# Two-layer hybrid decoder in fp32 on one core: expert down products in column groups of 64 and 32, weights in whole row blocks, small products in halves

## The chip, the cores and the metric

The program runs on one core of a Trainium2 chip. The metric is device time in microseconds (us) of one execution, median of three runs. All arithmetic is fp32.

## The reference, cut to what matters

The input has 256 tokens of width 1024. Two layers each do a norm, one input projection, four kinds of token mixing (sliding-window attention, gated linear attention, stick-breaking attention, RWKV-7), an output projection and a second norm. Layer 0 then has a dense SwiGLU of width 2816, layer 1 a mixture of eight experts, of which each token uses two:

```python
def swiglu(h, w1, w3, w2):
    return (jax.nn.silu(h @ w1) * (h @ w3)) @ w2

def moe_swiglu(h, router, w1, w3, w2):
    ...
    for e in range(N_EXPERTS):            # 8 experts, w1 and w3 (1024, 1408), w2 (1408, 1024)
        out = out + combine[..., e:e + 1].astype(h.dtype) * swiglu(h, w1[e], w3[e], w2[e])
    return out
```

## The kernel before, in words

Each engine has its own hand-written program; semaphores tie them together. There are eight PSUM banks of 128 partitions by 512 floats. For a bank b the semaphore `full[b]` counts how often TensorE has filled it and `free[b]` how often it has been read out; `nth(i, b, k)` is the k-th such count in expert pass i, from the list `per` of uses per pass. `mm(out, lhsT, rhs)` (L518) is one product: the columns of lhsT (at most 128) are loaded as weights and the columns of rhs (at most 512) stream through. Nearly every matmul of the kernel has L518 as its line. In the trace a product is always two MATMUL records and two LDWEIGHTS records; I call each of these a record. In a row, "128*64 128x96" is a weight block of 128 rows by 64 columns and 96 streamed columns.

**Experts** (`experts(l)`, layer 1). A pass handles up to CAP = 96 token slots of one expert; with these inputs the loop runs eight times. The tokens of the expert are gathered with a one-hot matrix, `gather`: for each of eight feature blocks and two token tiles, two products of 64 weight columns with 96 streamed columns, into banks 6 and 7. They are scaled out into `slot_h` (ScalarE four blocks, VectorE four). Then come the stages of a pass, in TensorE's order:

1. *Up*: for each of 11 blocks j of 128 expert features, first the gate (w1), then the up side (w3): over eight blocks k of the model width, two products, one for weight columns 0 to 63 of the block and one for 64 to 127, with 96 streamed columns. Their outputs go to partitions 0 to 63 and 64 to 127 of bank j % 2. That is 11 x 2 x 8 x 2 = 352 products, 704 records. ScalarE takes the silu of each block and VectorE multiplies (`slot_act`), one block at a time beside TensorE.
2. *Transposes*: two, of the weights of the slots (`weigh`), into bank 2; ScalarE copies them to `weigh_t`.
3. *Gather* of the next expert: 32 products, 64 records.
4. *Down*: for each block k of 11, the 96 slots of `slot_act[:, k]` are the weight block (96 columns) and w2 streams in two halves of 512 columns, into banks 2 and 3: 22 products, 44 records.
5. *Scatter*: four products of 512 streamed columns that put the result back to tokens, after ScalarE and VectorE have copied banks 2 and 3 to `slot_y`; VectorE adds each to `x_sb`.

**Weights of the experts.** SyncE issues 18 pieces for each pass, into nine slots of 128 x 2176 floats (six of `ring`, three in `region_e`). A piece of w1 or w3 is 256 columns of all eight row blocks, so each of its packets is 1 KB; a piece of w2 is two whole row blocks, with packets of 4 KB. A slot is refilled when TensorE is through with it. The pieces of a pass are 17.3 MB.

**Mixers** (`layer_mixers(l)`, once for each layer). Several products there have 128 weight columns and only 64 streamed ones: CO 12 products, GO 8, AO 12, right-hand sides RH0 4 and RH1 8, solves U0 4 and U1 4, outputs Y0 8 and Y1 12, so 72 in a layer. BON (4 in a layer) streams 2 columns and the router RT (16, in layer 1 alone) streams 8. They stand between other work of 128 weight columns; only GO is followed by products of 64 weight columns (L745 ff.). In `layer_mixers` the product LW (weight rows 0 to 63, input `d_th` in `region_m`) stands as four records ahead of the four records of LA (rows 64 to 127, input in `region_e`).

Of the kernel before, what the change touches and what calls it, by code (L numbers as in the profile page):

```python
# [9 lines left out]
ALU = mybir.AluOpType  # L10
# [3 lines left out]
P = 128  # L14
HALF = 64
D = 1024
# [37 lines left out]
MAX_PASSES = -(-SEQ // CAP)  # L54

# [84 lines left out]
def psum_plan():  # L140
# [9 lines left out]
    for l in range(DEPTH):  # L150
# [19 lines left out]
        if l % 2 == 0:  # L170
            for j in range(D_FF // P):
                use(f"up{j}", l, j % 2)
            for i in range(4):
                use(f"dn{i}", l, 2 + i)
        else:
            for name, bank in (("RT", 6), ("POS", 7), ("G0", 6), ("G1", 7)):
                use(name, l, bank)
# [16 lines left out]
def build(nc, t_in, out):  # L194
    ctx = ExitStack()
    with ctx:
# [13 lines left out]
        ring = sb("ring", [P, SLOTS, SLOT])  # L210
        region_e = sb("region_e", [P, 8192])
        region_f = sb("region_f", [P, 4096])
        region_g = sb("region_g", [P, 3072])
        region_m = sb("region_m", [P, 5128])
        normed = sb("normed", [P, 2, 512])
        ar = sb("ar", [P, 2, 2, NT, 256])
        c_q = sb("c_q", [P, 2, 2, SEQ])
        b_q = sb("b_q", [P, 4, SEQ])
        b_att = sb("b_att", [P, NT, 4, P])
        a_k = sb("a_k", [P, 2, SEQ])  # L220
# [85 lines left out]
        final_row = region_f[:, 1024:2048]  # L306

        W = MAX_PASSES * N_EXPERTS + N_EXPERTS
        slot_act = region_e[:, 0:UPC * CAP].rearrange("p (c s) -> p c s", c=UPC)
        slot_silu = region_f[:, 0:2 * CAP].rearrange("p (b s) -> p b s", b=2)  # L310
        slot_h = region_m[:, 0:KC * CAP].rearrange("p (c s) -> p c s", c=KC)
        pick = region_m[:, 768:768 + NT * CAP].rearrange("p (t s) -> p t s", t=NT)
        weigh = region_m[:, 960:960 + NT * CAP].rearrange("p (t s) -> p t s", t=NT)
        weigh_t = region_m[0:CAP, 1152:1152 + SEQ].rearrange("p (t n) -> p t n", t=NT)
        slot_y = region_m[0:CAP, 1408:1408 + D]
        place = region_m[:, 2432:2432 + NT * W].rearrange("p (t i) -> p t i", t=NT)
        chosen = region_m[:, 2432 + NT * W:2432 + 2 * NT * W].rearrange("p (t i) -> p t i", t=NT)
        share = region_m[:, 2432 + 2 * NT * W:2432 + 3 * NT * W].rearrange("p (t i) -> p t i", t=NT)
        count = region_m[:, 3072:3072 + N_EXPERTS]
        most = region_m[:, 3080:3088]  # L320
# [58 lines left out]
        def slot(n):  # L379
            return n % SLOTS  # L380


        MORE = 3
        SLOTS_E = SLOTS + MORE
        more_slots = region_e[:, 8192 - MORE * SLOT:8192].rearrange("p (s n) -> p s n", s=MORE)
        more_landed = [ctx.enter_context(nc.semaphore(f"more_slot{i}_landed")) for i in range(MORE)]

        def expert_slot(k, n):

            r = k % SLOTS_E  # L390
            return ring[:, slot(FIRST_MOE + r), 0:n] if r < SLOTS else more_slots[:, r - SLOTS, 0:n]

        def expert_landed(i, k):

            r = k % SLOTS_E
            before = (FIRST_MOE + r) // SLOTS if r < SLOTS else 0
            s = landed[slot(FIRST_MOE + r)] if r < SLOTS else more_landed[r - SLOTS]
            return s, i * (16 * (E_PIECES // SLOTS_E)) + 16 * (before + k // SLOTS_E + 1)

# [4 lines left out]
        E_PIECES = 3 * UP2  # L404
        assert E_PIECES % SLOTS_E == 0


        per = [(UPC + 1) // 2, UPC // 2, 3, 2, 1, 1, 1, 1]
# [12 lines left out]
        def _(sp):  # L421
# [42 lines left out]
            def expert_piece(e, k):  # L464
                if k < 2 * UP2:
# [1473 lines left out]
```

## Time and profile before

| | |
|---|---|
| median of 3 runs | 1143.51 us (1140.59 to 1144.64) |
| the profiled execution, its own time | 1143.13 us |
| its span, first to last instruction | 1141.3 us |
| TensorE busy | 1102.5 us (97%) |
| VectorE, ScalarE, GpSimd busy | 285.3, 192.9, 61.4 us |
| chain that ended last | TensorE 95%, VectorE 3% |
| eight expert passes | 689.3 to 1131.6 us |
| HBM read | 211.67 MB |

Times in rows are microseconds from the start of the span. A TensorE group of the timeline runs from the start of its first record to the modelled end of its last, so the groups overlap a little; distances from start to start are what counts. The chain is followed back from the last instruction: each step goes to what released it.

### The profile page before, as it was taken

The page shows a single profiled execution, that of the slowest core. Times are in us where ns is not written, and L with a number is a line of the kernel's source. Part 1 is how long each engine was busy: PE and PEld are TensorE (multiplying, and loading weights), DVE is VectorE, ACT ScalarE, POOL GpSimd, SP SyncE. Part 2 cuts the span into 40 slices and gives each one's busy share as a digit, 9 for nine tenths or more (in the row PEclk, how much of TensorE's full clock was granted, in tenths as well). Part 3 has the DMA queues.
Part 4 walks back from the last instruction along what each step waited for, and adds up shares of the span by engine and source line. Part 5 has one row for each costly group of instructions (what it writes and reads, how often), then busy time and mean ns, then how long its engine had stood idle before and what let it go on. Part 6 is the DMA issues. An engine that isn't in the chain of part 4 may idle for free.

```text
span 1141.3 us, 22432 instructions
## 1 busy us (share of the span) xinstructions
PE 1102.5 (97%) x9790; PEld 837.2 (73%) x9790; DVE 285.3 (25%) x645; ACT 192.9 (17%) x444; POOL 61.4 (5%) x67
## 2 busy tenths in 40 slices
PE   8999999899999999999999969999999999999996
PEld 6887887488888543887789549595949494949592
DVE  4432473500000001233376341020111112021112
ACT  2244231100000001214323011011010111101011
POOL 2000411000000000000312100000000000000000
PEclk8999999999999999999999989999999999999998
DMA  9633101335554445343210256989898989899870
GB/s 325 196 122 105 43 1 38 111 117 160 160 159 167 156 148 155 119 135 109 74 38 1 74 185 203 343 279 351 287 344 289 343 293 323 305 301 332 279 272 37
DMA packets 168650, 213.34 MB, mean 187 GB/s; under 512 B 5120, under 2 KB 151200, under 8 KB 168480
## 3 DMA queue, kind: packets, MB, share of 16 engines
q1 hardware_dynamic: 166032, 210.29, 56.0%
q10 hardware_dynamic: 2576, 2.45, 0.7%
q8 instruction: 32, 0.52, 0.2%
q14 instruction: 10, 0.08, 0.0%
HBM read 211.67 MB, written 1.05 MB: 186 GB/s over the span
## 4 chain that ended last, share of the span: by engine, by line
PE 95%; DVE 3%; issue 1%; ACT 1%; POOL 0%; DMA 0%; DVEq 0%; POOLq 0%; ACTq 0%
PE bank L518 93%; PE bank L523 1%; DVE tok L1434 1%; POOL small L1343 0%; DMA x_sb<-in_x 0%; DVE b_att L1616 0%; DVE b_q L1413 0%; PE bank L1045 0%; DVE x_sb L1410 0%; PE bank L829 0%; ACT tok L1121 0%; DVE small L1425 0%; ACT hT L1133 0%; DVE hT L1410 0%; PE bank L797 0%
## 5 line engine op out<-in xcount | busy, mean ns | idle before, releaser
L518 PE MATMUL bank<-hT,ring 128*128 128x256 f32 (+1 forms) x1184 | 260.3, 382 | 0.0
L518 PEld LDWEIGHTS bank<-hT,ring 128*128 128x128 f32 (+1 forms) x1184 | 223.4, 189 | 36.1 <-issue 2.7
L518 PEld LDWEIGHTS bank<-region_m,ring 128*64 128x64 f32 x4096 | 170.3, 137 | 8.6 <-issue 8.6
L518 PE MATMUL bank<-region_m,ring 128*64 128x96 f32 x4096 | 173.7, 246 | 2.9 <-DVE region_m L1860 1.6
L518 PE MATMUL bank<-ring,region_e 128*96 128x512 f32 (+1 forms) x368 | 160.0, 594 | 0.0
L518 PEld LDWEIGHTS bank<-ring,region_e 128*96 128x96 f32 (+1 forms) x368 | 64.1, 176 | 89.5 <-issue 88.5
L518 PE MATMUL bank<-ring,hT 128*128 128x256 f32 (+1 forms) x448 | 127.8, 442 | 1.4 <-ACT hT L1138 1.4
L518 PE MATMUL bank<-region_e 128*128 128x128 f32 (+2 forms) x512 | 119.2, 384 | 0.0
L1410 DVE TENSOR_TENSOR region_e<-region_f,bank 128x96 f32<-128x96 f32 (+1 forms) x110 | 31.7, 288 | 341.7 <-ACT region_f L1318 198.9
L518 PEld LDWEIGHTS bank<-ring,hT 128*128 128x128 f32 x448 | 84.0, 190 | 35.7 <-issue 25.8
L518 PEld LDWEIGHTS bank<-region_e 128*128 128x128 f32 (+1 forms) x512 | 71.9, 191 | 46.9 <-issue 46.8
L518 PE MATMUL bank<-region_m,region_e 128*64 128x96 f32 x1536 | 66.1, 246 | 0.0
L518 PEld LDWEIGHTS bank<-region_m,region_e 128*64 128x64 f32 x1536 | 64.4, 137 | 0.0
L1318 ACT ACTIVATE region_f<-bank 128x96 f32<-128x96 f32 x88 | 22.1, 251 | 234.8 <-PE bank L518 234.8
L1343 POOL TENSOR_TENSOR small<-small 128x1 f32<-128x1 f32 (+1 forms) x18 | 18.6, 1034 | 800.5 <-DVE small L1425 738.8
L1410 DVE TENSOR_TENSOR x_sb<-x_sb,bank 128x512 f32<-128x512 f32 x44 | 30.3, 689 | 93.5 <-PE bank L518 93.5
L518 PE MATMUL bank<-region_f 128*128 128x128 f32 (+1 forms) x352 | 43.0, 275 | 0.0
L518 PEld LDWEIGHTS bank<-region_f 128*128 128x128 f32 x352 | 41.2, 192 | 1.6 <-issue 1.6
L1880 DVE COPY region_m<-bank 96x512 f32<-96x512 f32 x8 | 5.5, 686 | 144.4 <-PE bank L518 144.4
L1296 ACT ACTIVATE region_f<-bank 128x256 f32<-128x256 f32 x22 | 8.4, 384 | 138.6 <-PE bank L518 138.6
L518 PE MATMUL bank<-region_m 96*128 96x512 f32 x64 | 30.4, 617 | 0.0
L523 PE MATMUL bank<-consts,tok 128*128 128x128 f32 x96 | 17.0, 323 | 13.5 <-DVE tok L1434 13.5
(234 smaller groups left out, 715.0 us busy)
## 6 DMA issues: line engine op xcount, KB each, us to landing
ring<-in_moe_w SPq DMA_DIRECT2D x80, 1024.0 KB, 6.9
region_e<-in_moe_w SPq DMA_DIRECT2D x40, 1024.0 KB, 6.8
ring<-in_ffn_w SPq DMA_DIRECT2D x33, 1024.0 KB, 5.4
ring<-in_w_in SPq DMA_DIRECT2D x22, 1024.0 KB, 5.4
ring<-in_w_out SPq DMA_DIRECT2D x8, 1024.0 KB, 4.9
ring<-in_moe_w SPq DMA_DIRECT2D x16, 512.0 KB, 5.8
region_e<-in_moe_w SPq DMA_DIRECT2D x8, 512.0 KB, 4.0
ring<-in_w_in SPq DMA_DIRECT2D x2, 1088.0 KB, 5.5
```

The lines of the kernel that those rows point to most:

```text
L518: return nc.tensor.matmul(o, lhsT, rhs, start=start, stop=stop, skip_group_check=True)
L523: last = nc.tensor.transpose(bank(name, l)[:, cc * 256 + t * P:cc * 256 + t * P + P], tok[:, t, (2 * c2 + cc) * P:(2 * c2 + cc + 1) * P], ...
L1296: nc.scalar.activation(silu_tmp[:, j % 2, :], bank(f"up{j}", l)[:, 0:SEQ], ACT.Silu).then_inc(sem("silu"), 1)
L1318: nc.scalar.activation(slot_silu[:, b, :], banks[b][:, 0:CAP], ACT.Silu).then_inc(sem("moe_silu"), 1)
L1343: g.tensor_tensor(ap_out, ap_in, m_half[:, 0:n], ALU.pow).then_inc(sem("rstd_ready"), 1)
L1410: return v.tensor_tensor(o, a, b, op)
L1434: v.tensor_scalar(tok[:, t, s], x_sb[:, t, s], scale, None, ALU.mult).then_inc(sem("h_ready"), 1)
L1880: v.tensor_copy(slot_y[:, 512:1024], banks[3][0:CAP, :]).then_inc(free[3], 1)
```

## The change

1. *Down in column groups.* The 96 slots are split into 64 and 32. For the first 64 slots a product has 64 weight columns and 512 streamed ones (`down_wide`), one for each half of w2: the first goes to array columns 0 to 63 and partitions 0 to 63 of bank 5, the second to columns and partitions 64 to 127 of bank 6. For the last 32 slots a product has 32 weight columns and 256 streamed ones (`down_narrow`), four of them in four groups of 32 array columns. In blocks k = 0 to 7 both kinds follow each other; for k = 8, 9, 10 (TAIL) all narrow ones come first, then the wide ones.
2. *Order of a pass*: up, transposes, down, gather, scatter. The transposes use bank 5, which down uses too, so down now waits for ScalarE's copy `weigh_t`. The scatter uses banks 1 to 4.
3. *Up with k outermost.* All 22 blocks accumulate together in banks 0 to 4, so silu and multiplication come at the end of the stage, five blocks (480 columns) in one instruction.
4. *Weights.* Sixteen row blocks `rows_a` (w1 and w3, 128 rows x 1408 columns, packets of 5.6 KB) and `rows_b` (w2, six transfers with packets of 4 KB) hold a whole expert. They lie in one `arena` over all mixer buffers. A row block is refilled for the next expert when TensorE is through with it. For the first expert, rows 9 and up and all of w2 wait for `x_updated`, the others for ring slots.
5. *Small products in halves* (`mm_halves`): the mixer products named above and the router's are split into two of 64 weight columns. The number of products and records of up and gather stays the same.

```diff
+def mm_halves(o, lhsT, rhs, start=False, stop=False):
+    for q in range(0, P, HALF):
+        last = mm(o[q:q + HALF, :], lhsT[:, q:q + HALF], rhs, start=start, stop=stop)
+    return last
...
-                    mm(o[:, h * HD:(h + 1) * HD], a0[:, hh, 0:P], c_v[:, 0, v], start=(h == 0), stop=True)
+                    mm_halves(o[:, h * HD:(h + 1) * HD], a0[:, hh, 0:P], c_v[:, 0, v], start=(h == 0), stop=True)
...
-        per = [(UPC + 1) // 2, UPC // 2, 3, 2, 1, 1, 1, 1]
+        GATE = [(0, j * CAP) if j < 5 else (1, (j - 5) * CAP) if j < 10 else (4, 0) for j in range(UPC)]
+        UP = [(2, j * CAP) if j < 5 else (3, (j - 5) * CAP) if j < 10 else (4, CAP) for j in range(UPC)]
+        per = [2, 2, 2, 2, 2, 3, 2, 1]
...
             with sp.Fori(0, n * N_EXPERTS - 1) as i:
+                for k in range(ROWS_A):
+                    if k < ROWS_A - 2:
+                        sp.wait_ge(sem("moe_row_used"), i * (KC - 1) + k // 2 + 1)
+                    else:
+                        sp.wait_ge(full[3], nth(i, 3, 1))
+                    expert_row_a((i + 1) % N_EXPERTS, k)
+                for b in range(ROWS_B):
+                    if b < ROWS_B - TAIL:
+                        sp.wait_ge(sem("moe_w2_used"), i * (ROWS_B - TAIL) + b + 1)
+                    else:
+                        sp.wait_ge(full[6], nth(i, 6, 2))
+                    expert_rows_b((i + 1) % N_EXPERTS, b)
...
+                def down_wide(k, g):
+                    return mm(banks[5 + g][g * HALF:(g + 1) * HALF, :], slot_act[:, k, 0:HALF],
+                              rows_b[:, k, g * 512:(g + 1) * 512], start=(k == 0), stop=(k == UPC - 1))
+                def down_narrow(k):
+                    for c in range(4):
+                        last = mm(banks[6 - c // 2][c * QUARTER:(c + 1) * QUARTER, 0:GW], slot_act[:, k, HALF:CAP],
+                                  rows_b[:, k, c * GW:(c + 1) * GW], start=(k == 0), stop=(k == UPC - 1))
+                        if k == UPC - 1 and c % 2:
+                            last.then_inc(full[6 - c // 2], 1)
+                    return last
...
                 with pe.Fori(0, n_passes * N_EXPERTS) as i:
+                    pe.wait_ge(free[7], nth(i, 7, 0))
+                    pe.wait_ge(free[0], nth(i, 0, 0))
+                    for k in range(KC):
+                        pe.wait_ge(a_landed[2 * k], 16 * i + 16)
+                        for j in range(5):
+                            last = up_tile(GATE[j], k, 2 * k, j, k == 0 and j == 0)
...
+                    pe.wait_ge(sem("weighs"), i + 1)
+                    pe.wait_ge(free[5], nth(i, 5, 0))
+                    for t in range(NT):
+                        last = nc.tensor.transpose(banks[5][0:CAP, t * P:(t + 1) * P], weigh[:, t, :], ident)
+                    last.then_inc(full[5], 1)
+
+                    pe.wait_ge(free[5], nth(i, 5, 1))
                     pe.wait_ge(free[6], nth(i, 6, 0))
+                    for k2 in range(ROWS_B):
+                        pe.wait_ge(b_landed[k2], 16 * i + 16)
+                        if k2 == 0:
+                            pe.wait_ge(free[2], nth(i, 2, 1))
...
+                        if k2 < ROWS_B - TAIL:
+                            for k in (2 * k2, 2 * k2 + 1):
+                                for g in range(2):
+                                    down_wide(k, g)
+                                last = down_narrow(k)
+                            last.then_inc(sem("moe_w2_used"), 1)
+                    for k in range(2 * (ROWS_B - TAIL), UPC):
+                        down_narrow(k)
+                    for k in range(2 * (ROWS_B - TAIL), UPC):
+                        for g in range(2):
+                            last = down_wide(k, g)
...
                     pe.wait_ge(sem("picks"), i + 2)
+                    gather((nth(i, 7, 0), nth(i, 0, 1)))
+                    for b, t, half in SCATTER:
+                        if half == 0:
+                            pe.wait_ge(free[5], nth(i, 5, 3))
+                        else:
+                            pe.wait_ge(free[6], nth(i, 6, 2))
+                        pe.wait_ge(free[b], nth(i, b, 1))
...
+                        for b in (0, 1):
+                            act.wait_ge(full[b], nth(i, b, 1))
+                            nc.scalar.activation(slot_silu[:, 5 * b:5 * b + 5, :],
+                                                 banks[b][:, 0:5 * CAP].rearrange("p (c s) -> p c s", c=5),
+                                                 ACT.Silu).then_inc(free[b], 1)
...
+                        act.wait_ge(full[5], nth(i, 5, 1))
+                        nc.scalar.copy(weigh_t, banks[5][0:CAP, 0:SEQ].rearrange("p (t n) -> p t n", t=NT)).then_inc(
+                            free[5], 1)
...
-SCATTER = ((4, 0, 0), (5, 0, 1), (2, 1, 0), (3, 1, 1))
+SCATTER = ((1, 0, 0), (2, 1, 0), (3, 0, 1), (4, 1, 1))
```

## Rows read from the trace of the kernel before

**Rows 1.** The page: chain that ended last, shares of the span by engine.
```profile
PE 95%; DVE 3%; issue 1%; ACT 1%; POOL 0%; DMA 0%; DVEq 0%; POOLq 0%; ACTq 0%
```

**Rows 2.** The same chain in order of time: start, length, what.
```profile
689.28 25.54 PE bank L518 x613
714.82 1.37 issue
...
775.64 54.73 PE bank L518 x820
```

**Rows 3.** Timeline of TensorE in one expert pass: start, us, engine, group.
```profile
746.02 16.06 PE L518 MATMUL bank<-region_m,ring 128*64 128x96 f32 x384
...
771.15 4.13 PE L518 MATMUL bank<-region_m,ring 128*64 128x96 f32 x96
775.21 0.42 PE L1045 MATMUL bank<-consts,region_m 128*96 128x128 f32 x2
775.57 2.86 PE L518 MATMUL bank<-region_m,tok 128*64 128x96 f32 x64
778.36 10.54 PE L518 MATMUL bank<-ring,region_e 128*96 128x512 f32 x24
788.74 8.75 PE L518 MATMUL bank<-region_e 128*96 128x512 f32 x20
797.37 3.80 PE L518 MATMUL bank<-region_m 96*128 96x512 f32 x8
801.11 1.13 PE L518 MATMUL bank<-region_m,ring 128*64 128x96 f32 x22
```

**Rows 4.** Timeline of TensorE, LW (region_m) and LA (region_e), layer 1.
```profile
481.90 0.48 PE L518 MATMUL bank<-region_m,lora 64*128 64x256 f32 x1
481.91 0.48 PE L518 MATMUL bank<-region_e,lora 64*128 64x256 f32 x1
...
482.65 0.38 PE L518 MATMUL bank<-region_m,lora 64*128 64x256 f32 x1
482.66 0.38 PE L518 MATMUL bank<-region_e,lora 64*128 64x256 f32 x1
```

**Rows 5.** Timeline of TensorE around gated attention's scores, which alternate column halves.
```profile
576.48 0.44 PE L708 MATMUL bank<-consts,hT 128*128 128x128 f32 x2
576.85 1.08 PE L518 MATMUL bank<-b_q,hT 128*64 128x256 f32 x8
577.87 0.60 PE L518 MATMUL bank<-region_e 128*128 128x128 f32 x3
```

**Rows 6.** Timeline of all engines, end of up to start of down.
```profile
775.67 0.37 ACT L1321 COPY region_m<-bank 96x256 f32<-96x256 f32 x1
777.15 1.04 ACT L1303 ACTIVATE region_m<-bank,params 128x96 f32<-128x96 f32 x4 [1.11 <-PE bank L518]
```

**Rows 7.** Timeline of all engines, end of down and the scatter.
```profile
796.66 0.58 ACT L1328 COPY region_m<-bank 96x512 f32<-96x512 f32 x1 [18.47 <-PE bank L518]
797.36 0.30 PEld L518 LDWEIGHTS bank<-region_m 96*128 96x128 f32 x2 [0.74 <-issue]
797.52 0.69 DVE L1880 COPY region_m<-bank 96x512 f32<-96x512 f32 x1 [18.05 <-PE bank L518]
798.53 0.69 DVE L1410 TENSOR_TENSOR x_sb<-x_sb,bank 128x512 f32<-128x512 f32 x1 [0.32 <-PE bank L518]
```

**Rows 8.** Busy time by stretch, one expert pass: engines, clock, DMA share, GB/s.
```profile
746.00:801.10 55.10, 55.10 (x823) 40.36 (x822) 8.29 (x24) 6.03 (x18) 0.00 (x0) 1.00 0.94 316
```

**Rows 9.** DMA in 780 to 790 us (w1, w3 pieces) and 765 to 775 (w2).
```profile
DMA packets 3448, 3.48 MB, mean 348 GB/s; under 512 B 48, under 2 KB 3448, under 8 KB 3448
...
DMA packets 1030, 3.96 MB, mean 396 GB/s; under 512 B 63, under 2 KB 63, under 8 KB 1030
```

**Rows 10.** Timeline of TensorE: AO of layer 1 and what follows.
```profile
618.93 2.79 PE L518 MATMUL bank<-region_m,hT 128*128 128x64 f32 x24
621.56 0.66 PE L518 MATMUL bank<-region_e 128*128 128x128 f32 x4
```

**Rows 11.** Timeline: the router's products.
```profile
671.22 4.85 PE L518 MATMUL bank<-router_sb,hT 128*128 128x8 f32 x32 [1.05 <-ACT hT L1133]
```

More of the change, by code:

```diff
@@ L15 @@
 HALF = 64
+QUARTER = 32
+TAIL = 2
 D = 1024
@@ L1042, in experts @@
-                    pe.wait_ge(sem("weighs"), i + 1)
-                    pe.wait_ge(free[2], nth(i, 2, 0))
-                    for t in range(NT):
-                        last = nc.tensor.transpose(banks[2][0:CAP, t * P:(t + 1) * P], weigh[:, t, :], ident)
-                    last.then_inc(full[2], 1)
-                    pe.wait_ge(sem("picks"), i + 2)
-                    gather(i, (nth(i, 6, 0), nth(i, 7, 0)))
-                    pe.wait_ge(free[2], nth(i, 2, 1))
-                    pe.wait_ge(free[3], nth(i, 3, 0))
@@ L1314, in _ @@
                     with act.Fori(0, n_passes * N_EXPERTS) as i:
-                        for j in range(UPC):
-                            b = j % 2
-                            act.wait_ge(full[b], nth(i, b, j // 2 + 1))
-                            nc.scalar.activation(slot_silu[:, b, :], banks[b][:, 0:CAP],
-                                                 ACT.Silu).then_inc(sem("moe_silu"), 1)
-                        act.wait_ge(full[2], nth(i, 2, 1))
-                        nc.scalar.copy(weigh_t, banks[2][0:CAP, 0:SEQ].rearrange("p (t n) -> p t n", t=NT)).then_inc(
-                            free[2], 1)
@@ new lines, in _ @@
+                        nc.scalar.activation(slot_silu[:, 10, :], banks[4][:, 0:CAP],
+                                             ACT.Silu).then_inc(sem("moe_silu"), 1)
+                        act.wait_ge(full[5], nth(i, 5, 1))
+                        nc.scalar.copy(weigh_t, banks[5][0:CAP, 0:SEQ].rearrange("p (t n) -> p t n", t=NT)).then_inc(
+                            free[5], 1)
+                        act.wait_ge(full[6], nth(i, 6, 1))
+                        for c in range(2):
+                            last = nc.scalar.copy(slot_y[HALF:CAP, c * GW:(c + 1) * GW],
+                                                  banks[6][c * QUARTER:(c + 1) * QUARTER, 0:GW])
@@ L1324, in _ @@
+                        last.then_inc(free[6], 1)
+                        act.wait_ge(full[5], nth(i, 5, 3))
+                        nc.scalar.copy(slot_y[0:HALF, 0:512], banks[5][0:HALF, :]).then_inc(free[5], 1)
+                        act.wait_ge(full[7], nth(i, 7, 1))
                         for c in range(4):
-                            last = slots_in(c, 6)
-                        last.then_inc(free[6], 1)
-                        act.wait_ge(full[2], nth(i, 2, 2))
-                        nc.scalar.copy(slot_y[:, 0:512], banks[2][0:CAP, :]).then_inc(free[2], 1)
+                            last = slots_in(c, 7)
@@ L1329, in _ @@
+                        last.then_inc(free[7], 1)
             square_sums(2 * DEPTH)
```

304 lines of the change are left out of this document (149 added, 155 removed).

## Prediction, made before the changed kernel was run

> **What bounds the kernel now.** I read the page's chain first: TensorE holds 95% of it [rows 1]. The chain in order of time then says where its work is back to back. From 720.55 to 1131.71 us there are only TensorE records, 54.73 us to an expert pass; the one wait is 1.37 us in the first pass [rows 2]. The timeline splits a pass [rows 3]. It lasts 801.11 - 746.02 = 55.09 us: up 29.19 (to 775.21), transposes 0.36, gather 2.79, down 19.01, scatter 3.74. So a microsecond that TensorE loses or gains in a pass counts eight times. DMA is busy for 0.94 of a pass [rows 8], but nobody waits for it after the first one.
>
> **How a product is paid.** In down a record streams 512 columns in 19.01 / 44 = 0.43 us, that is 0.84 ns a column. In up 608 records lie between 746.02 and 771.15 [rows 3], 41 ns each, where 96 columns alone would take 80 ns: two products in different array columns run at the same time. The scores of gated attention show it for 256 columns: 8 records in about 0.86 us, 0.108 each, where 0.215 would be due alone [rows 5]. And the order is loose. LA's four records stand behind LW's four in the program, yet its first starts 0.01 us after LW's first and its last 0.01 after LW's last [rows 4]. So records queued for another part of the array pass those that wait for their own.
>
> A change of the column width costs extra. Gather has 64 records x 0.041 = 2.64 us of work and takes 2.79; the transposes have 2 x 0.1075 of 0.36 [rows 3]; around the scores it is 0.37 - 0.215 and 1.02 - 0.86 [rows 5]. That is 0.14 to 0.16 us for each change, the unhidden first weight load included.
>
> **Part 1, down.** Before: 19.01 us, with 96 of the 128 array columns in use. After, for each k: wide, two products of two records of 0.43, the two products abreast, 0.86 us; narrow, four products of two records of 0.215, four abreast, 0.43 us. Eleven k make 11 x 1.29 = 14.19 us. The unknown is the change between column widths of 64 and 32. Blocks 0 to 7 change 8 times to narrow and 7 times back, and the tail changes once: 16. The trace has no such change. The nearest rows are the changes between 64 and 96 or 128 columns, 0.14 to 0.16 with a first load of 64 to 128 columns in them [rows 3, 5]; loads of 32 and 64 columns are shorter, so I take 0.14, and as ends 0 (no drain between these two) and 0.18. So 16 x 0.14 = 2.24, down 16.43 us, **2.58 less in a pass**.
>
> This is where a rule speaks against the change. Column width 64 and 128 cost 0.15 us at each border here [rows 3]. The Trainium skill, page "TensorEngine Tiling (Array Packing)", section "Key Properties", says that changing the tiling mode, not just the tile, drains TensorE. By that rule all 16 changes are paid (down 16.4); without it none (14.2). The trace agrees for the widths that it has.
>
> **Part 2, the order of a pass.** Up to transposes, transposes to down, gather to scatter, scatter to up: four changes of width as before, down to gather has none, as gather to down had one. Down now waits for the copy of `weigh_t`. ScalarE began it 0.46 us after the transposes began and took 0.37 [rows 6]; with 0.1 for the semaphore TensorE goes on 0.93 us after 775.21 instead of 0.36: **+0.57**. Queued behind that wait are down and everything else of TensorE. ScalarE must be free for it: its last silus cover 96 and 480 columns; a 512-column copy takes 0.58 [rows 7], and the last bank of the gate side is full 1.65 us (40 records x 0.041) before up ends. That holds. VectorE multiplies 480 columns in about 0.69 [rows 7]; bank 2 is full 0.83 before up ends, so it is done before the copy; bank 3 is first needed four k later. Up to +0.4 if the silus come late. After down, gather's 2.64 us cover the copies to `slot_y` (0.58 and 0.69 [rows 7]); the 0.1 us which the scatter now loses at such a wait goes, and so does a first load, **-0.14**. The scatter's 3.6 us cover the scaling of the next slots (1.04 [rows 6]). VectorE's additions (0.69 each [rows 7]) free banks 1 to 4 in the order in which up asks for them; the fourth ends about 1 us into up, which asks for bank 4 only after 40 records (1.65 us). Nothing.
>
> **Part 3, up with k outermost.** The same 704 records; 29.19 us stays. Nothing (bounds: 0 to 0.3 for a few waits).
>
> **Part 4, weights.** With packets of 1 KB the DMA moved 348 GB/s at full share, with 4 KB 396 [rows 9]. A pass of 52.9 us needs 17.3 MB / 52.9 = 327 GB/s, below both; a row block is refilled nearly a whole pass ahead of its use. The first pass took 746.02 - 689.28 = 56.74 us, 1.65 more than the others [rows 2, 3]; that wait for weights goes, because SyncE queues everything by 666 us and 17.3 MB at 396 GB/s arrive long before their turn: **-1.7**. If not, 0.
>
> **Sum for the experts.** A pass: -2.58 + 0.57 - 0.14 = -2.15; eight: -17.2; with the first pass -18.9 us.
>
> **Part 5, halves.** AO's 24 records take 621.56 - 618.93 = 2.63 us, 0.11 each, though 64 columns stream in 0.054 [rows 10]: the load of 128 weight columns sets the pace. As halves each load is half as long, and up shows that the loads of the two halves run side by side (two serial ones of 0.055 would not fit a pair's 0.082 [rows 3]). So four records in 0.112 us instead of two in 0.223, -0.111 a product; the upper end of the pace is up's own, 0.041 a record, -0.058 a product. An excursion from width 128 to 64 and back costs 0.33 us: two drains of 0.09 and the first loads of 0.05 and 0.10. GO needs none, since 64-column products follow it. In a layer: CO, AO, Y1 (12 each) -1.0; GO -0.9; Y0, RH1 (8 each) -0.56; RH0, U0, U1 (4 each) -0.1; BON 0. That is -5.3, or -1.4 at the upper pace; two layers -10.6 or -2.8. The router's 16 products (4.85 us, partly at a lower clock [rows 11]) bring -1.4 or -0.6. Small waits take some of it, since other engines' chains then end last; I take **-10**, ends -12 and -3. The nearest row to small moving widths is up, whose pairs show parallel loads, so I stay near the lower end.
>
> **Total.** Against the profiled execution's own 1143.13 us (its span is 1141.3): -18.9 - 10 = 1114.2. That execution lies 0.4 us below the median, so 1114.6.
>
> **Rivals.** (a) *No drain between 64 and 32.* All 16 changes are free; another 8 x 2.24 = 18 us go: 1097 us. For it: both are column groups that keep all rows. Against it: every change of width in the trace is paid [rows 3, 5].
>
> (b) *Slower: the four narrow products do not run four abreast but two.* Then narrow costs 0.86 a k, down is 11 x 1.72 + 2.24 = 21.2 us, a pass grows by 2.15 + 0.57 - 0.14 = 2.6, eight by 21, and with -1.7 - 10 the sum is 1152.5. The side changes where the narrow k costs 0.43 + 28.9 / 88 = 0.76, some 2.3 abreast. For it: nothing in the trace runs more than two abreast, and were a record to start only after the one ahead of it, two records of one product would block the next group. Against it: rows 4, where records four places behind start with the first. The Trainium skill, page "TensorE: Matmul & The Clock Gate", section "The mechanism", says that matmuls keep strict program order; rows 4 disagree. By that rule the wide products still pair up, the narrow ones too, and this rival's time comes out.
>
> (c) *The gains are there but small*: changes at 0.18 us (16 x 8 x 0.04 = 5.1), late silus (8 x 0.4 = 3.2), the mixers at -3 (7): 1114.6 + 15.3 = 1130. This is the upper edge of the forecast.
>
> **Chances.** Forecast with its bounds (1105 to 1130) 0.68; (a), 1093 to 1103, 0.14; (b) 0.11; within 0.3% for other reasons 0.04; between 1130 and 1140 0.03. Range: 1097 to 1130. About 0.3% is what a measurement of this kernel tells from no change. Faster 0.85, same 0.04, slower 0.11.
>
> **What would show it.** In the timeline of a pass: up 29.2; 0.9 from transposes to down; down 16.4 (14.2 for (a), 21.2 for (b)), with 1.57 us from one k's first wide record to the next's; gather 2.7; scatter 3.6; a pass of 52.9. Narrow records start in fours for the forecast and in twos for (b). A product in the mixers: four records in 0.11 us. The first pass no longer than the others. The prediction is wrong if a width of 32 costs more than 0.36 us a change, where the sum is nil, if up runs slower with its outputs spread over five banks, or if TensorE waits for a multiplication at the end of up.

## The result, and the profile after

| | before | after |
|---|---|---|
| median of the runs beside each other | 1142.89 us (4 runs, 1140.59 to 1144.64) | 1172.94 us (4 runs, 1168.8 to 1176.66) |
| the profiled execution, its own time and span | 1143.13, 1141.3 us | 1176.66, 1174.6 us |
| start of the expert loop | 689.3 us | 675.8 us |
| one expert pass, from transposes to transposes | 55.09 us | 59.3 to 65.0 us |

The ratio is 1.0263, with a 95% interval of 1.0223 to 1.0303: the change makes the kernel slower by 30 us, where I forecast 29 us faster.

The page of after, the lines that answer to rows 1 and to the table of before. The line PEclk is the clock that TensorE was granted, in 40 slices of the span, in tenths of full speed. The line q8 is a DMA queue: packets, MB, share of 16 engines' span. The last line is the chain that ended last.

```profile
span 1174.6 us, 24084 instructions
PE 1093.0 (93%) x10830; PEld 819.1 (70%) x10830; DVE 281.2 (24%) x597; ACT 186.9 (16%) x396; POOL 61.3 (5%) x67
...
PEclk9999999999999999999999799898999898989899
...
q8 instruction: 98, 1.61, 0.5%
...
PE 91%; issue 4%; DVE 2%; ACT 1%; POOL 0%; DMA 0%; DVEq 0%; POOLq 0%; ACTq 0%
```

"issue" has gone from 1% of the chain [rows 1] to 4%: TensorE stands still and no semaphore explains it. The chain in order of time says where (start, length, what), from the start of the expert loop:

```profile
675.80 11.93 PE bank L525 x283
688.00 5.50 PE bank L525 x128
694.20 5.50 PE bank L525 x128
700.39 5.50 PE bank L525 x128
709.40 22.99 PE bank L525 x204
732.39 2.20 issue
734.59 1.80 PE bank L525 x28
737.31 18.45 PE bank L525 x383
756.74 5.50 PE bank L525 x128
```

In before the same view had one stop of 1.37 us, behind 613 records, and then 54.73 us without a gap in every pass [rows 2]. Here TensorE stops behind 283 records, then behind every 128, and at each jump back to the start of the loop; there it stops again behind 28. Compare rows 3 with a whole pass of after, the timeline of TensorE (start, us, engine, group, and in brackets the idle time before it):

```profile
799.75 2.09 PE L525 MATMUL bank<-arena 128*64 128x96 f32 x28 [2.35 <-issue]
803.09 18.21 PE L525 MATMUL bank<-arena 128*64 128x96 f32 x383 [1.26 <-issue]
822.00 12.29 PE L525 MATMUL bank<-arena 128*64 128x96 f32 x293 [0.70 <-issue]
834.22 0.42 PE L1088 MATMUL bank<-consts,arena 128*96 128x128 f32 x2
835.42 16.72 PE L525 MATMUL bank<-arena 128*64 128x512 f32 x132 [0.78 <-ACT arena L1375]
851.97 2.81 PE L525 MATMUL bank<-arena,tok 128*64 128x96 f32 x64
854.71 3.70 PE L525 MATMUL bank<-arena 96*128 96x512 f32 x8
861.43 0.88 PE L525 MATMUL bank<-arena 128*64 128x96 f32 x10 [3.02 <-issue]
```

Down, the subject of the change, takes 851.97 - 835.42 = 16.55 us, as I had forecast (16.4). Yet the pass lasts 861.43 - 799.75 = 61.68 us. Of that, 1.26 + 0.70 + 3.02 = 4.98 us are stops with "issue" as their reason. Another part is the clock, by the view of busy time in two stretches (us, TensorE busy with its records, granted clock, DMA share, GB/s):

```profile
800.09:806.91 6.82, 5.56 (x75) 0.51 0.02 5
806.91:820.00 13.09, 13.00 (x313) 0.99 0.83 314
```

From 800.2 us TensorE runs at half its speed, 1.2 GHz instead of 2.4, for 6.8 us; ahead of it stood the stop of 2.35 us, and within it, behind 28 records, the one of 1.26. By the same view in steps of 0.5 us such stretches begin at 735.4, 800.2, 861.7, 923.1, 984.6, 1046.0 and 1107.4 us. Six last 6.8 us, the third 3.4. Five begin within 1.3 us behind the first record of a pass, the last two already in the stop ahead of it. In before the clock stays at 1.00 over a pass [rows 8].

**Where the 33.3 us of span came from.** The loop starts 689.28 - 675.80 = 13.5 us earlier. It lasts 1164.93 - 675.80 = 489.1 us instead of 1131.71 - 689.28 = 442.4, 46.7 more, and what follows is as long as before: -13.5 + 46.7 = 33.2. My sum had the loop at 8 x 52.93 = 423.5, so 65.6 are to be explained. The stops are in the view of waits, over 675 to 1165 us (total, times, longest):

```profile
PE bank L525 <- issue: 39.7, 31, 3.6
```

The stages without stops add up to 53.34 us a pass, 0.41 above the sum, so 8 x 0.41 = 3.3 us. The granted clock is at half for 6 x 6.8 + 3.4 = 44.2 us. Stops take 8.4 of these and are counted already; of the other 35.8 half is lost, 17.9. Together 60.9. The 4.7 us left over are about what the view of waits leaves out: a group of 128 records lasts 5.50 us up to the modelled end of its last, where 128 records of an unstopped up take 128 x 29.19 / 704 = 5.31, so by this estimate each of the 31 stops costs some 0.2 us more than it shows.

### The profile page after: what moved, and what is told of

It reads as the page before. It is cut to its first block, busy times and chain, and to the rows that moved or that the text cites. A ratio compares the mean times of both kernels' runs of the same rounds, so it can differ in the third digit from the quotient of the medians.

```text
span 1174.6 us, 24084 instructions
## 1 busy us (share of the span) xinstructions
PE 1093.0 (93%) x10830; PEld 819.1 (70%) x10830; DVE 281.2 (24%) x597; ACT 186.9 (16%) x396; POOL 61.3 (5%) x67
## 3 DMA queue, kind: packets, MB, share of 16 engines
q8 instruction: 98, 1.61, 0.5%
## 4 chain that ended last, share of the span: by engine, by line
PE 91%; issue 4%; DVE 2%; ACT 1%; POOL 0%; DMA 0%; DVEq 0%; POOLq 0%; ACTq 0%
PE bank L525 89%; PE bank L536 1%; DVE tok L1493 1%; POOL small L1402 0%; DMA x_sb<-in_x 0%; DVE arena L1675 0%; DVE arena L1472 0%; ACT arena L1375 0%; PE bank L1088 0%; DVE x_sb L1469 0%; PE bank L842 0%; ACT tok L1172 0%; DVE small L1484 0%; ACT hT L1184 0%; DVE hT L1469 0%
## 5 line engine op out<-in xcount | busy, mean ns | idle before, releaser
L525 PE MATMUL bank<-arena 128*64 128x96 f32 (+5 forms) x8128 | 620.1, 295 | 48.2 <-issue 40.7
L525 PEld LDWEIGHTS bank<-arena 128*64 128x64 f32 (+2 forms) x8128 | 437.6, 146 | 224.8 <-issue 217.4
L525 PE MATMUL bank<-hT,arena 128*128 128x256 f32 (+1 forms) x1184 | 259.2, 381 | 0.0
L525 PEld LDWEIGHTS bank<-hT,arena 128*128 128x128 f32 (+1 forms) x1184 | 222.6, 189 | 35.8 <-issue 2.7
L1469 DVE TENSOR_TENSOR arena<-arena,bank 128x512 f32<-128x512 f32 (+3 forms) x90 | 51.2, 577 | 424.2 <-ACT arena L1372 261.4
L525 PE MATMUL bank<-arena,hT 128*128 128x256 f32 (+4 forms) x572 | 137.8, 404 | 5.1 <-DVE arena L1675 3.7
L525 PEld LDWEIGHTS bank<-arena,hT 128*128 128x128 f32 (+2 forms) x572 | 89.7, 179 | 42.2 <-issue 26.2
L1189 ACT COPY arena<-bank 128x512 f32<-128x512 f32 (+2 forms) x66 | 37.4, 567 | 165.7 <-PE bank L525 159.6
L1469 DVE TENSOR_TENSOR arena<-arena 128x512 f32<-128x512 f32 (+3 forms) x50 | 31.3, 646 | 28.2 <-ACT arena L1189 27.4
L525 PE MATMUL bank<-arena,tok 128*64 128x96 f32 x576 | 27.4, 257 | 1.2 <-DVE arena L1842 1.2
## 6 DMA issues: line engine op xcount, KB each, us to landing
consts<-in_consts SPq DMA_DIRECT2D x1, 1377.0 KB, 11.3
```

The costliest lines, as they stand in the source:

```text
L525: return nc.tensor.matmul(o, lhsT, rhs, start=start, stop=stop, skip_group_check=True)
L1189: frees(nc.scalar.copy(dst, src), name, l)
L1469: return v.tensor_tensor(o, a, b, op)
```

## Experiments

**The theories.** (A) *The instructions of the loop no longer fit.* The stops come in steps of 128 records, that is 128 weight-load and 128 matmul records, 256 instructions; and the queue named "instruction" moves packets of 1.61 MB / 98 = 16.4 KB, one for each such block (64 bytes an instruction). Over 735 to 1105 us, six passes, the DMA view has

```profile
q8 instruction: 52, 0.85, 0.9%
```

for after, 52 / 6 = nearly nine a pass, and none of this queue for before. Where the block borders lie follows from where TensorE stopped: with each instruction of its program counted from the start, before's stop behind 613 records and after's behind 283, 411, 539, 667 and, in later passes, 28 records all agree with borders at 242 (plus or minus 2) modulo 256. Before's loop has 822 x 2 + 47 waits and register operations = 1691 instructions and starts at 6934, so it lies in blocks 26.14 to 32.74, which are seven. After's has 910 x 2 + 28 = 1848 and starts at 7606, so 28.77 to 35.98, which are eight. By (A) a loop in seven blocks is read once and kept, one in eight is fetched anew in every pass. The length of the loop counts as well as where it starts, and every instruction ahead of the loop moves the start: the halves of part 5 add 672.

(B) *The new down or the larger blocks of weights do it*: narrow products, loads of 32 columns, the waits for `weigh_t`, or packets of weights that crowd out other DMA. Then undoing them must cure it and moving the loop must not.

(C) *TensorE's clock* falls for a reason of its own, and the stops are its shadow.

### Part 5 alone, and code that only moves the loop

`halves_only`: before, with nothing but the halves, in BON, CO, GO, AO, RH, U, Y and RT. Expert code, weights and order are those of before.

```diff
+            def mm_halves(o, lhsT, rhs, start=False, stop=False):
+                for q in range(0, P, HALF):
+                    last = mm(o[q:q + HALF, :], lhsT[:, q:q + HALF], rhs, start=start, stop=stop)
+                return last
...
-                        last = mm(bank("RT", l)[:, t * N_EXPERTS:(t + 1) * N_EXPERTS], hT[:, k, t * P:(t + 1) * P],
+                        last = mm_halves(bank("RT", l)[:, t * N_EXPERTS:(t + 1) * N_EXPERTS], hT[:, k, t * P:(t + 1) * P],
```

> The kernel before with part 5 alone: the mixers' and the router's small products in halves. Experts, weights and their order are those of before. The halves add 672 instructions in front of the expert loop, so the loop of 1691 instructions starts at another place of TensorE's program: counted in blocks of 256 instructions from the places where TensorE stopped in the changed kernel, it now touches 8 blocks instead of 7. Theory A (a loop that touches more than 7 blocks is read anew from memory in every pass, and TensorE waits for it): the mixers gain about 13 us as in the changed kernel, but each pass after the first takes 59 to 65 us instead of 55.1, with fetches in every pass; about 1165 to 1200 us in all. Theory B (the changed kernel waits for its expert weights, which come as late row blocks): passes stay at 55.1 us, 1142.9 - 13.5 = 1129 us. Theory C (only the length of the loop counts, somewhere between 1691 and 1848 instructions): also 1129 us.

Measured: 1180.0 us (4 runs), ratio 1.0329 (1.0301 to 1.0356). Its page, and its chain at the jumps back of two passes:

```profile
q8 instruction: 98, 1.61, 0.6%
```

```profile
734.27 4.16 issue
738.43 2.51 PE bank L518 x28
...
796.76 3.10 issue
799.86 2.51 PE bank L518 x28
```

Loop 7606 to 9296, blocks 28.77 to 35.37: eight. The whole loss is there, more than all of after's, with the old down and the old weights. (B) falls. A pass is 799.86 - 738.43 = 61.4 us of a loop that has not been touched. The loop starts at 679.12 us, 10.2 earlier than in before.

`before_shift110`: before, with 110 instructions more at the start of TensorE's program, waits on a semaphore that has long been reached (two waits become one instruction: the page counts 22542 instructions where before's has 22432).

```diff
             pe.wait_ge(sem("ident_landed"), 16)
+            for _ in range(220):
+                pe.wait_ge(sem("zeros"), 1)
```

> The kernel before with 110 satisfied waits put into TensorE's program near its start, nothing else. The expert loop is the same 1691 instructions but touches 8 blocks of 256 instead of 7. Theory A: passes of 59 to 65 us with a fetch for every block in every pass, 1175 to 1220 us in all. Theories B and C: passes stay at 55.1 us, and the waits cost at most 6 us at the start: 1143 to 1149 us.

Measured: 1176.29 us (2 runs), ratio 1.0293 (1.0266 to 1.032). Blocks 26.57 to 33.17: eight. Not one product differs from before. The page and the chain:

```profile
q8 instruction: 60, 0.98, 0.3%
```

```profile
724.78 54.73 PE bank L518 x820
...
805.40 4.13 issue
...
843.37 26.67 PE bank L518 x139
```

The distances between the transposes of one pass and the next are 55.08, 63.5, 55.08, 64.77, 55.08, 65.92, 55.08: every second pass fetches, the others do not. (A) as told above has every pass fetch, so it is right on the border and not on this. The 110 instructions stand in a gap of 5.96 us of TensorE near the start, but before waits there too, and the loop starts only 691.13 - 689.28 = 1.85 us later. The three slow passes cost 8.4 + 9.7 + 10.8 us and everything up to the first transposes 724.43 - 720.13 = 4.3 more: 33.2, the whole difference of the two profiled executions.

`before_shift256`: the same with 512 waits, 256 instructions, one whole block.

> The control: the kernel before with 256 satisfied waits near TensorE's start, a whole block, so that the loop touches 7 blocks as before. Theories A, B and C all expect passes of 55.1 us and no fetch after the first pass; the waits cost up to 13 us at the start, so 1143 to 1156 us. If passes are long here too, theory A's count of blocks is wrong.

Measured: 1160.87 us (2 runs), ratio 1.0158 (1.013 to 1.0186). Blocks 27.14 to 33.74: seven again. More instructions are added than in the run above, and behind the first pass the stops are gone:

```profile
q8 instruction: 33, 0.54, 0.2%
```

```profile
739.02 54.73 PE bank L518 x820
...
794.11 54.73 PE bank L518 x820
```

The passes are 55.08 us. What is left is the price of the waits: the loop starts at 708.85 us, 19.6 later than in before, where I had reckoned 13. TensorE stands from 8.49 to 30.14 us at them.

`halves_shift68`: `halves_only` with 68 instructions of waits (`range(136)`), which move the loop to 7674.

> The kernel before with the mixers' and the router's small products in halves, and 68 satisfied waits near TensorE's start, which put the start of the expert loop 8 instructions behind the start of a block: 7 blocks touched. Theory A: passes of 55.1 us and no fetch after the first pass, 1129 us plus up to 4 us for the waits, far below the same kernel without the 68 waits. Theories B and C: the same 1129 to 1133 us, and no difference to the kernel without the waits.

Measured: 1131.81 us (4 runs), ratio 0.9896 (0.9865 to 0.9927). Blocks 29.03 to 35.63: seven.

```profile
q8 instruction: 35, 0.57, 0.2%
```

```profile
681.82 29.26 PE bank L518 x704
711.44 54.73 PE bank L518 x820
766.52 54.73 PE bank L518 x820
```

So 68 instructions that do nothing take 48.2 us off `halves_only`. (C) falls too: the granted clock is 1.00 from 735 to 1105 us here and 0.94 in `halves_only` (busy time by stretch), on the same work, so the clock follows the stops. And part 5 by itself is worth what was forecast: 1131.81 against 1143.16 is 11.3 us, the waits paid, which put the loop at 681.82 us instead of 679.12.

### The new down, with a loop that fits and one that doesn't

`fit7`: after, with 80 instructions fewer in the loop, which now starts at 7418: the gather (64 instructions) and four products of up whole, and so are BON, U0, U1 and RH0 in the mixers; four instructions of waits ahead of the loop set the start.

```diff
-                                last = mm_halves(banks[b][:, c * CAP:(c + 1) * CAP],
+                                last = mm(banks[b][:, c * CAP:(c + 1) * CAP],
...
+                    whole = k == KC - 1 and row % 2 == 1 and 6 <= j < 10
+                    return (mm if whole else mm_halves)(banks[b][:, at:at + CAP], rows_a[:, row, j * P:(j + 1) * P], slot_h[:, k, :],
```

> The changed kernel with its expert loop shortened from 1848 to 1768 instructions and moved so that it touches 7 blocks of 256 instead of 8: the gather's 16 block products and the last four block products of up are whole (128 weight columns, two records of 0.112 us instead of four of 0.041); the products of BON, U0, U1 and RH0 in the mixers are whole again; four satisfied waits before the router's positions. Down, the order of a pass and the weights are those of the changed kernel. Theory A (a loop that touches more than 7 blocks is read anew in every pass): no fetch after the first pass and no wait for one; a pass is 29.4 up, 1.15 to down, 16.55 down, 3.6 gather, 3.7 scatter, 54.4 us; about 1124 us in all. Theory B (expert weights come late): the waits of 8 to 12 us in a pass stay, about 1175 to 1180 us.

Measured: 1130.01 us (4 runs), ratio 0.9895 (0.9847 to 0.9943); loop of 1768 instructions, blocks 28.03 to 34.93: seven. A pass is 54.47 us, as expected, of which down is 16.65; the total is 6 us above what I expected. The whole gather costs 3.65 instead of 2.74. From 735 to 1105 us no stop is put down to "issue", with the new down and the new blocks of weights in place: what is left of (B) falls too.

`fit7_tail6`: the same with `TAIL = 6`: narrow and wide products alternate in no block. All narrow ones of k = 0 to 10 come first, which leaves one change between 64 and 32 columns instead of sixteen.

```diff
-TAIL = 2
+TAIL = 6
```

> The kernel of fit7 with TAIL 6 instead of 2: in down all narrow products of the eleven k come first, then all wide ones, so the column width changes once instead of 16 times. Theory A with 0.14 us for a change: down 16.55 - 15 x 0.14 = 14.4 us, a pass of 52.3 us, 1107 us in all. If a change cost nothing between 64 and 32 columns, down would stay at 16.5 and the time at that of fit7. Theory B: late weights would get worse, as all of w2 is released only at the end of down: over 1175 us.

Measured: 1118.9 us (4 runs), ratio 0.978 (0.9753 to 0.9807). The timelines of the two, `fit7` first:

```profile
822.30 16.72 PE L525 MATMUL bank<-arena 128*64 128x512 f32 x132 [0.76 <-ACT arena L1378]
838.95 3.81 PE L525 MATMUL bank<-arena,tok 128*128 128x96 f32 x32
```

```profile
821.01 14.55 PE L525 MATMUL bank<-arena 128*32 128x256 f32 x132 [1.14 <-DVE arena L1472]
835.49 3.81 PE L525 MATMUL bank<-arena,tok 128*128 128x96 f32 x32
```

Down goes from 16.65 to 835.49 - 821.01 = 14.48 us; 15 changes gone for 2.17 us, **0.14 us each**. Starting with the narrow products brings a wait of 1.14 us instead of 0.76, for a multiplication of VectorE. The total is 12 us above the 1107 expected: half of that is the 6 that `fit7` was above its own, 8 x 0.4 = 3 is this wait, and the loop starts 2.4 us later than in `fit7`.

`after_shift68`: after, with 136 waits (68 instructions) between the router and the loop, which moves it to 7674.

> The changed kernel with 68 satisfied waits before the router's positions, which puts the start of its expert loop at the start of a block. The loop of 1848 instructions is longer than 7 blocks (1792) and touches 8 wherever it starts. Theory A (8 blocks touched): still slow, 1165 to 1180 us. A theory A' in which only the place of the loop's start counts: passes of 53.3 us, about 1118 us. Theory B: 1173 us.

Measured: 1159.05 us (5 runs, 1150.43 to 1160.73), ratio 1.0129 (1.0095 to 1.0163), lower than I expected. At 1848 instructions the loop spans 29.03 to 36.25, still eight blocks. The same 68 instructions that cured `halves_only` do not cure it. Its profiled execution is the fastest, 1150.43 us. It loses less than after: the stops in 735 to 1105 us are 22.0 us instead of 31.9, and the granted clock there is 0.98 instead of 0.95.

`old_down`: after, with down as 22 products of 96 slots again (into banks 5 and 6), one copy of 96x512 each by ScalarE and VectorE, all else kept, and the 68 instructions of waits.

```diff
+                        for half in range(2):
+                            for k in range(2 * k2, min(2 * k2 + 2, UPC)):
+                                last = mm(banks[5 + half][0:CAP, :], slot_act[:, k, :],
+                                          rows_b[:, k, half * 512:(half + 1) * 512], start=(k == 0),
+                                          stop=(k == UPC - 1))
```

> The changed kernel with the down stage of before (one product of 96 weight columns and 512 streamed ones for each half and k, 44 records), everything else as changed, and 68 satisfied waits before the router's positions: a loop of 1670 instructions that touches 7 blocks. Theory A: no waits for instructions; a pass is 29.2 + 1.15 + 19.0 + 2.8 + 3.7 = 55.8 us, about 1134 us in all. So down in column groups would be worth 2.5 us a pass by its profile, and the new order would cost 0.7. Theory B: the late row blocks stay late, over 1150 us.

Measured: 1141.53 us (10 runs), ratio 0.9984 (0.9966 to 1.0002); 1670 instructions, blocks 29.03 to 35.55: seven. A pass is 55.82 us, as expected. The total is 7 us above what I expected, since the loop starts at 682.06 us, 6.3 later than in after; 3.69 of that is the waits, which hold TensorE up ahead of the loop; for the rest I have no cause (in `after_shift68`, with the same program ahead of the loop, it starts at 679.40). Down takes 19.05 us here and 16.55 in after, so the column groups are worth 2.5 us a pass. Against before's 55.09 the pass shows what parts 2 to 4 cost: 0.73 us. The sum had the wait for `weigh_t` at 0.57 less 0.14; with the 0.2 by which that wait is longer (below) it is 0.63.

### The faster version, with and without the alignment

`best`: as in `fit7` the gather inside the loop and four products of up whole, `TAIL = 6` with the narrow products of a row block behind its wait, all halves in the mixers, and 68 instructions of waits where TensorE waits anyhow, in the first layer's transposes.

```diff
+ALIGN = 68
...
+                    if l == 0 and which == 0 and t == 1:
+                        for _ in range(2 * ALIGN):
+                            pe.wait_ge(sem("zeros"), 1)
...
+                        for k in range(2 * k2, min(2 * k2 + 2, UPC)):
+                            down_narrow(k)
```

> The kernel of fit7_tail6 with three repairs: TensorE waits for the fourth to tenth multiplied blocks just before the narrow product that reads them, not before all of down; the first gather and all mixer products are in halves again; the 68 satisfied waits that put the loop's start (1768 instructions) at a block's start stand near the start of the kernel, where TensorE waits 4 us for VectorE. 7 blocks touched. Theory A: a pass of 52.71 - 0.38 = 52.3 us, the loop starting at about 677 instead of 682 us, 1110 us in all, and no fetch of instructions after the first pass. Theory B (weights come late in the changed kernel): over 1140 us.

Measured: **1114.82 us** (5 runs, 1111.49 to 1115.98), ratio 0.9739 (0.9718 to 0.9761). Loop of 1768 instructions from 7674, blocks 29.03 to 35.93: seven. The chain and a pass of the timeline:

```profile
767.72 51.34 PE bank L526 x868
...
820.01 51.35 PE bank L526 x868
```

```profile
820.01 14.55 PE L526 MATMUL bank<-arena 128*32 128x256 f32 x132 [0.73 <-ACT arena L1380]
834.49 3.81 PE L526 MATMUL bank<-arena,tok 128*128 128x96 f32 x32
```

A pass is 820.01 - 767.72 = 52.29 us, as expected. The total is 5 us above the 1110 expected: the loop starts at 682.60 us, not at 677 (677.03 in `best_unaligned`, below). The router takes 1.55 us of that, 3.59 at a granted clock of 0.50 instead of 2.04 at 1.00; whether the waits cost the rest was not told apart.

`best_unaligned`: the same with `ALIGN = 0`; every product and its order is the same.

> The kernel of best without the 68 waits at its start: the same loop of 1768 instructions, shorter than 7 blocks of 256, but touching 8. Theory A: fetches in every pass or in every second one, 25 to 60 us more than best. Theory C (only the loop's length counts): the time of best.

Measured: 1187.92 us (2 runs), ratio 1.0388 (1.0367 to 1.041). Blocks 28.77 to 35.67: eight.

```profile
800.06 1.38 PE L526 MATMUL bank<-arena 128*64 128x96 f32 x28 [1.80 <-issue]
806.42 18.40 PE L526 MATMUL bank<-arena 128*64 128x96 f32 x383 [4.98 <-issue]
```

```profile
PE bank L526 <- issue: 47.8, 25, 5.0
```

(the second fence is the view of waits, 735 to 1105 us.) The same products in the same order take 1115 or 1188 us, by where their loop begins.

### What a fetch costs without the weights' traffic

`no_reload`: after, without the transfers of expert weights behind the first expert's (SyncE's loop over the experts is gone). It leaves out that each expert has its own weights: all eight passes use those of expert 0.

```diff
-            with sp.Fori(0, n * N_EXPERTS - 1) as i:
...
-                        pe.wait_ge(a_landed[2 * k], 16 * i + 16)
+                        pe.wait_ge(a_landed[2 * k], 16)
```

> The changed kernel without the transfers of expert weights after the first expert: all experts are computed with the weights of expert 0, so its output is another; TensorE's program keeps its place and length (8 blocks touched). It tells whether the weights' traffic is part of the cost of a fetch. Theory A with fetches that queue behind weight packets: 9 fetches in a pass remain, but the waits for them (8 to 11 us in a pass of the changed kernel) shrink to 0 to 3 us, 1120 to 1140 us in all. If fetches are slow by themselves, the waits stay and the time is near 1170 us. Theory B (waits for weights): no waits at all, 1119 us.

Measured, in one run: 1132.84 us. The fetches stay, eight blocks being eight; the page has the 98 packets of after. The stops shrink, by the waits and the timeline of the same stretch as above:

```profile
PE bank L512 <- issue: 12.1, 12, 1.8
```

```profile
792.67 28.11 PE L512 MATMUL bank<-arena 128*64 128x96 f32 x676 [1.69 <-issue]
...
845.13 1.38 PE L512 MATMUL bank<-arena 128*64 128x96 f32 x28 [0.29 <-issue]
847.93 12.29 PE L512 MATMUL bank<-arena 128*64 128x96 f32 x293 [1.42 <-issue]
```

12.1 us of stops instead of 31.9, passes of 55.0 to 55.7 us, and no stretch at half clock. Every pass behind the first still stops behind the first 28 records of up, for 1.15 to 1.78 us; at the jump back the stop is at most 0.47 us, and at the later borders of up there is none. One execution of one kernel shows it, but the stops differ by more than twice. So a block costs time mostly because it shares the DMA with the weights: beside them, one comes every 6.2 us (688.00, 694.20, 700.39), and up uses one in 5.5.

## Why the prediction was wrong, point by point

**The terms that held.** Down: 16.55 us against 16.43; from one k's first wide record to the next's 1.58 against 1.57. The weight loads of after show both kinds, wide in fours and narrow in eights:

```profile
709.39 0.20 PEld L525 LDWEIGHTS bank<-arena 128*64 128x64 f32 x4 [0.98 <-issue]
710.41 0.16 PEld L525 LDWEIGHTS bank<-arena 128*32 128x32 f32 x8 [0.81 <-issue]
710.98 0.20 PEld L525 LDWEIGHTS bank<-arena 128*64 128x64 f32 x4 [0.41 <-issue]
```

From the first wide load to the first narrow one 1.02 us, which is 0.86 of streaming and a change; then 0.57, which is 0.43 and a change. So the narrow products do run four abreast, and rival (b) falls; `fit7_tail6` prices a change at 0.14 us, my value, and rival (a) falls. Gather 2.74 (2.7), scatter 3.7 (3.6), up 29.2 where it isn't stopped. Part 5 alone brings the loop forward by 10.2 us in `halves_only`, where I took 10. Four records of a mixer product take at most 0.135 us (AO's 48 in 1.62) where I had 0.11. After's 13.5 us are more than part 5 explains, and part of them is luck: the router's 64 records take 2.04 us there at a granted clock of 1.00, but 3.59 at 0.50 in `halves_only`, against 4.85 at 0.74 for before's 32 [rows 11]. At full clock that is 2.04 / 64 = 32 ns a record, below the 41 of up that I had taken for the upper pace. The rest of the 3.3 us was not taken apart.

**A term that was short.** From the transposes to down 709.40 - 708.25 = 1.15 us, not 0.93: TensorE goes on later behind ScalarE's copy than the 0.1 us I gave the semaphore. 0.2 us a pass, 1.8 in all.

**The step that failed** is the first one, "What bounds the kernel now", and with it part 3. I read the chain as TensorE's products back to back and took the one wait that did not fit, 1.37 us in the first pass, for a wait for weights. It was no such wait. It is behind 613 records, five records into the up side of block j = 9, and TensorE waits for both pieces of that block ahead of j = 8, so no piece of weights begins there; a block of instructions does, and "issue" says that no semaphore was seen. Had I asked where it stood, I would have had a border of the blocks, and the count of 1691 instructions against 1848 would have followed from the diff. Part 3 gave "the same 704 records" in up no price, right for the records; but down grows from 44 to 132 records, 176 instructions (157 with 19 waits fewer), and the halves put 672 more ahead of the loop. I never counted instructions: all my terms were times of records, as if their code were always at hand. The gain that went into "the first pass -1.7" is the same error: the first pass of after has stops of 0.27 + 0.70 + 0.70 + 0.70 us, behind 283, 411, 539 and 667 records, where blocks of its code begin. In the terms of the sum, the stops, the half clock and what hangs on them stood at nothing; they took 489.1 - 8 x 53.34 = 62.4 us.

**The rivals.** I had given 0.11 to slower, all of it to a mechanism in the array. The true one was none of my rivals: a cost that lies in no instruction but in their number.

Worked out, not measured: without these 62.4 us after's profiled execution would have taken some 1114 us, where the forecast was 1114.6. That it comes so near is in part luck: the passes are 0.41 us longer than forecast, 3.3 in all, the start of the loop is 3.5 us earlier, and the two cancel. What was measured is `best`, with down faster by 2 us a pass and the gather slower by 0.9: 1114.82.

**What stays open.** Why `before_shift110` fetches in every second pass only, where all other loops of eight blocks do in each. Whether the border "seven fit, eight do not" is one of blocks kept or of blocks kept less the one fetched ahead was not told apart; nine packets a pass speak for the second. And which of two things lets `after_shift68` lose less than after, fewer instructions behind the last border or a better place of the stops, was not tried. Why the clock fell behind the stops of after and not behind the shorter ones of `no_reload` is not explained either.

## What to carry to other kernels

Count instructions as you count microseconds: a loop on the engine that sets the time has a size in code, and an edit anywhere ahead of it can move it across a border. In the profile look at the packets of the instruction queue inside the loop and at every wait that "issue" ends: stops at equal counts of instructions are code, not data. If a kernel gets slower by several per cent from an edit whose own rows are all as reckoned, shift the loop by some dozens of instructions before blaming the edit.

## What the runs showed of the hardware that I had not expected

- **TensorE keeps a loop of seven blocks of 256 instructions and refetches one of eight**, in every pass of five kernels and in every second one of `before_shift110`. Seven blocks, in 735 to 1105 us: no packets in before, passes of 55.08 us; eight: 52 packets in after, and 48 us more in the total for the same work in `halves_only` against `halves_shift68`, 73 in `best_unaligned` against `best`.
- The Trainium skill, page "Runtime: NRT & Kernel Launch", section "Instruction fetch mechanics", gives TensorE 2048 instructions of instruction memory, refilled in blocks of 256, and calls the crossing of a block mostly hidden. The packets of 16.4 KB and the stops behind every 128 records agree with the block; that a loop of eight blocks, 2048 instructions, doesn't stay agrees with it only if a part is taken up by the block fetched ahead. The crossing is not hidden here: in after's first pass TensorE stops for 0.27 to 0.70 us at each of four borders, in before's for 1.37 at one. The same section of the Trainium skill also lets a jump hit without a fetch only within two blocks; before jumps back over seven without one packet, so the measurement decides against that.
- **A jump back to a block that must be fetched** stops TensorE for 2.2 to 3.6 us in after, up to 4.6 in `halves_only`, and around it the granted clock falls to 1.2 GHz, for 6.8 us in six of seven passes of after. In `no_reload` the stops there are at most 0.47 us, those behind the next 28 records at most 1.8, and the clock does not fall.
- **Four products of 32 weight columns run abreast**, 8 records of 256 streamed columns in about 0.43 us, and going between groups of 32 and of 64 columns costs 0.14 us.
- **Waits are not free**: TensorE stood for 3.7 us at 68 instructions of waits already met just ahead of the loop and for 5.96 us at 110 near the start of the program, 0.054 us each; at 256 in the same place it stood for 21.65 us, 0.085 each. What that puts the loop off by depends on what TensorE waits for anyhow: 1.85 us for the 110, 19.6 for the 256.
